# Two layers of a diffusion backbone: fp32 hidden blocks during selection and gates, and 96 expert rows fetched early

## The reference, cut to what matters

```python
q = (x @ wq).reshape(n, 8, 2, 128)
s = einsum('nhcd,hckd->nhck', q, sub_keys)      # 128 keys for each of 8 heads and 2 halves
s1, i1 = top_k(s[:, :, 0], 16); s2, i2 = top_k(s[:, :, 1], 16)
cand = (s1[..., :, None] + s2[..., None, :])    # 16 x 16 pairs
top, pos = top_k(cand, 16); idx = i1*128 + i2   # 16 experts of 16384 for each token and head
gate = softmax(top)
act = gelu(einsum('nd,nhkd->nhk', x, u_tab[idx]), approximate=False)
y = einsum('nhk,nhkd->nd', gate * act, v_tab[idx])
```

## Time and profile before

| | us |
|---|---|
| median of 3 runs (lowest, highest) | 5162.43 (5157.72, 5165.9) |
| the profiled execution | 5158.91 |
| its span | 5157.1 |

### The profile page before, as it was taken

One profiled execution on the slowest core, in us unless ns is written; L12 is line 12 of the kernel. 1 busy time (PEld: TensorE's weight loads), 2 busy tenths in 40 slices (PEclk: granted clock), 3 DMA queues, 4 the chain that ended last, 5 costly groups with the idle time before them and its releaser, 6 DMA issues. The chain is left out here.

```text
span 5157.1 us, 78818 instructions
## 1 busy us (share of the span) xinstructions
PE 4192.3 (81%) x29134; PEld 3640.1 (71%) x29134; DVE 3765.5 (73%) x6707; ACT 1603.1 (31%) x2322; POOL 1497.4 (29%) x1046
## 2 busy tenths in 40 slices
PE   6975996888788888888778579869887788888886
PEld 4944775888777777777668257759876777777775
DVE  2245664369997999999932567533999799999997
ACT  3133542323242222222231435232333322222223
POOL 0000000000005777777600000000000076777774
PEclk8986987999998999999989779789999999999998
DMA  5140001223379999999921400011334799999996
GB/s 195 61 158 12 2 2 35 78 82 124 106 224 362 408 409 409 406 409 409 361 67 49 154 4 2 2 69 49 116 122 144 244 401 409 409 403 409 409 409 249
DMA packets 398567, 1079.12 MB, mean 209 GB/s; under 512 B 37248, under 2 KB 176768, under 8 KB 394752
## 3 DMA queue, kind: packets, MB, share of 16 engines
q1 hardware_dynamic: 250880, 539.10, 29.2%
q0 software_dynamic: 147456, 536.94, 26.3%
HBM read 996.47 MB, written 79.43 MB: 209 GB/s over the span
## 5 line engine op out<-in xcount | busy, mean ns | idle before, releaser
L1912 POOL DMA_INDIRECT ring<-peer_u_rows,rows x512 | 732.1, 1430 | 2756.7 <-issue 1333.4
L196 PE MATMUL ps<-vhi,wlo 128*128 128x512 f32 x1536 | 655.5, 427 | 276.0 <-DVE wlo L2056 275.4
L1912 POOL DMA_INDIRECT ring<-peer_v,rows x512 | 743.1, 1451 | 252.0 <-DVE acc L2074 166.1
L196 PE MATMUL ps<-hhi,ulo 128*128 128x384 f32 x2048 | 713.4, 348 | 102.1 <-DVE ulo L1473 97.8
L198 PE MATMUL ps<-hhi,uhi 128*128 128x384 f32 x2048 | 701.7, 343 | 0.0
L197 PE MATMUL ps<-hlo,uhi 128*128 128x384 f32 x2048 | 701.4, 342 | 0.0
L2074 DVE SCALAR_TENSOR_TENSOR acc<-ring,act,acc 128x1024 f32<-128x1024 f32 x512 | 660.1, 1289 | 23.1 <-DMA ring<-peer_v,rows 3.4
L2065 DVE SCALAR_TENSOR_TENSOR ring<-ring,acc 128x1024 f32<-128x1024 f32 x512 | 620.2, 1222 | 55.7 <-DMA ring<-peer_u_rows,rows 48.6
L197 PE MATMUL ps<-vlo,whi 128*128 128x512 f32 x1536 | 644.5, 420 | 0.0
L198 PE MATMUL ps<-vhi,whi 128*128 128x512 f32 x1536 | 640.8, 417 | 0.0
L196 PEld LDWEIGHTS ps<-vhi,wlo 128*128 128x128 f32 x1536 | 317.4, 207 | 369.5 <-issue 292.0
(11 more groups left out here) (333 smaller groups left out, 7844.2 us busy)
## 6 DMA issues: line engine op xcount, KB each, us to landing
u<-peer_u SPq DMA_DIRECT2D x256, 512.0 KB
v<-peer_v SPq DMA_DIRECT2D x256, 512.0 KB
gates<-stage SPq DMA_DIRECT2D x24, 2048.0 KB, 9.6
gw<-gates SPq DMA_DIRECT2D x64, 768.0 KB
mod_ring<-mod_late SPq DMA_DIRECT2D x16, 2048.0 KB, 8.8
hidden<-hh SPq DMA_DIRECT2D x128, 192.0 KB, 1.9
ha<-hidden SPq DMA_DIRECT2D x128, 192.0 KB
proj_raw<-w_proj SPq DMA_DIRECT2D x42, 512.0 KB, 3.6
```

Of the source, the lines that this page charges most:

```text
L196: pe.matmul(out, lhs[1], rhs[0], start=start, stop=False)
L1912: pool.indirect_dma_start(ring[:, m % RING, :], None, table, rows).then_inc(row_in[m % RING], 16)
```

## The change

- `u` gets a ring of four slots (`U_RING`). In selection and gates the three fp32r products of a chunk become one plain fp32 product of the raw `u` and the raw normed tokens, which are kept as one fp32 tensor `h`. `u_high` and `u_low` are gone from both stages. `h2` lives only through the query stage; the experts stage splits `h` again into `x2` (384 tokens) at its start.
- From the second tile of selection on, GpSimd gathers 96 `peer_u` rows of the first gathered tile (`DOTS_AHEAD`, own ring of 8) and DVE multiplies them out, 24 in each of tiles 1 to 4, at places written out by hand (`dots`). The tokens are turned for that during tile 0 (`tokens_first`), on TensorE and ScalarE.
- The two reductions at line 1708 become halving additions of the one-hot tensor (8, 4, 2, then 1).
- The experts stage has 416 rows left, 13 in each turn. Rows of the two tiles alternate in the `peer_v` part (`row_of`), the first of them writes the accumulator (no memset), and DVE's 32 turns are written out instead of looped.

```diff
+        self.u = g.sb(st, "u", [P, U_RING, KC, P])
...
     def products(self, pe, slot, bank, chunks):
         for kc in chunks:
-            mm = split3(pe, self.g.ps[:, slot, 0:ND], [x[:, slot, kc, :] for x in self.u2],
-                        [x[:, kc, 0:ND] for x in self.g.h2], start=(kc == 0), stop=(kc == KC - 1))
+            mm = pe.matmul(self.g.ps[:, bank, 0:ND], self.u[:, slot, kc, :], self.x[:, kc, 0:ND], start=(kc == 0), stop=(kc == KC - 1))
...
+DOTS_AHEAD = 96
+SELECT_RING = 8
...
+        @block.gpsimd
+        def _(pool):
+            pool.wait_ge(listed, 1)
+            for m in range(DOTS_AHEAD):
+                if m >= SELECT_RING:
+                    pool.wait_ge(used, m - SELECT_RING + 1)
+                own.gather(pool, d["peer_u_rows"], 0, m, ring[:, m % SELECT_RING, :]).then_inc(row_in[m % SELECT_RING], 16)
...
             for t in range(TILES):
                 for p, n in blocks(t):
-                    hid.hidden(pe, n, n % 2, first=n < 2)
-                    if p == 1 and t >= 1:
+                    hid.hidden(pe, n, n // U_RING + 1, first=n < 2)
+                    if t == 0 and p in (1, 3):
+                        tokens_first(p // 2)
+                    if p == 3 and t >= 1:
                         turned(t - 1)
-                    if p == 3 and t + 1 < TILES:
+                    if p == 6 and t + 1 < TILES:
                         scores(t + 1)
...
-                    if p == 5:
+                    if p == 8:
                         act.wait_ge(dif, t + 1)
                         nc.scalar.activation(res[:, 2, :, :], res[:, 2, :, :], ACT.Exp).then_inc(ex, 1)
...
+            each_tile = DOTS_AHEAD // (TILES - 1)
+            def dots(t, a, b):
+                for m in range((t - 1) * each_tile + a, (t - 1) * each_tile + b) if t >= 1 else ():
+                    ve.wait_ge(row_in[m % SELECT_RING], 16 * (m // SELECT_RING + 1))
+                    own.dot(ve, ring[:, m % SELECT_RING, :], 0, m).then_inc(used, 1)
...
-                    if o == NO - 1:
-                        hid.u_low(ve, t + (N0 + 2), q)
...
+DOTS = SPARSE * P - DOTS_AHEAD
+ROWS = DOTS + SPARSE * P
+PER_TURN = ROWS // NG
+LEAD = 13
...
+def row_of(m):
+    if m < DOTS:
+        return divmod(DOTS_AHEAD + m, P)
+    m -= DOTS
+    if m < LEAD:
+        return 0, m
+    if m < 2 * P - LEAD:
+        half, x = divmod(m - LEAD, 2)
+        return x, half + LEAD * (1 - x)
+    return 1, m - P
```

More of the change, by code:

```diff
@@ L1512, in __init__, with gather, dot @@
         self.act = [g.sb(st, "act", [P, P]) for _ in range(SPARSE)]
+        self.acc = g.sb(st, "acc", [P, SPARSE, D])
+        self.g = g
     def row_numbers(self, ve, k, x, first, second, base):
         k.then(ve.scalar_tensor_tensor(self.act[x][:, :], first, float(NKEY), second, ALU.mult, ALU.add))
-        k.did(ve.tensor_scalar(self.rows[x][:, :], self.act[x][:, :], base, None, ALU.add))
+        k.then(ve.tensor_scalar(self.rows[x][:, :], self.act[x][:, :], base, None, ALU.add))
+    def gather(self, pool, table, x, slot, to):
+        rows = bass.IndirectOffsetOnAxis(self.rows[x][:, slot:slot + 1], 0)
+        return pool.indirect_dma_start(to, None, table, rows)
+    def dot(self, ve, row, x, slot):
+        return ve.scalar_tensor_tensor(row, row, 1.0, self.acc[:, x, :], ALU.mult, ALU.mult, accum_out=self.act[x][:, slot:slot + 1])
+DOTS_AHEAD = 96
+SELECT_RING = 8
 def select_stage(g, l, qT, sel, kt, loaded, hid, own):
@@ L1531, in select_stage @@
     lists = g.sem("sel_lists_done")
+    turned_h, tok_ready, listed, used = (g.sem(f"ahead_{x}") for x in ("h_turned", "h_ready", "rows_listed", "rows_used"))
+    row_in = [g.sem(f"ahead_gathered{i}") for i in range(SELECT_RING)]
+    g.gathers += row_in
     NC = 2 * PH
@@ L1752, in turns @@
         def turns(eng, body):
[L1754 to L1758, removed]
+            with eng.Fori(0, TG // U_RING - 1) as i:
+                for q in range(U_RING):
+                    body(i * U_RING + q, q, i, False)
+            for q in range(U_RING):
+                body(TG - U_RING + q, q, TG // U_RING - 1, True)
         @block.vector
@@ L1904, in _ @@
             tables = d["peer_u_rows"], d["peer_v"].rearrange("l i (j d) -> (l i j) d", d=D)
[L1905 to L1912, removed]
-                        m += 1
+            for m in range(ROWS):
+                if m >= RING:
+                    pool.wait_ge(used, m - RING + 1)
+                own.gather(pool, tables[m >= DOTS], *row_of(m), ring[:, m % RING, :]).then_inc(row_in[m % RING], 16)
         @block.sync
@@ L1993, in _, with x_high, u_high @@
         def _(act):
+            def x_high(half):
+                kc = slice(half * KC // 2, (half + 1) * KC // 2)
+                nc.scalar.activation(x2[0][:, kc, :], hid.x[:, kc, 0:ND], ACT.Copy).then_inc(x_hi, 1)
+            def u_high(i, b, first=False):
+                act.wait_ge(hid.u_in[b], i * 16 + 16 * (AHEAD // U_RING + 1))
+                if not first:
+                    act.wait_ge(hid.h_ready, i * 2 + (AHEAD + b - 1))
+                nc.scalar.activation(u2[0][:, b, :, :], hid.u[:, b, :, :], ACT.Copy).then_inc(u_hi, 1)
             def v_high(i, j):
@@ L2069, in value, with weights_of @@
-            def value(x):
-                def row(i, q):
-                    r = gathered(i, q)
-                    ve.wait_ge(used, i * PER_TURN + q)
-                    w = own.act[x][:, bass.ds((i - (SPARSE + x) * DOT_TURNS) * PER_TURN + q, 1)]
-                    ve.scalar_tensor_tensor(acc[:, x, :], r, w, acc[:, x, :], ALU.mult, ALU.add).then_inc(used, 1)
-                return row
-            def turn(i, last, row):
-                def rows(*which):
-                    for q in which:
-                        row(i, q)
+            def weights_of(x):
+                ve.wait_ge(acted, x + 1)
+                ve.tensor_tensor(own.act[x][:, :], own.act[x][:, :], own.share[x][:, :], ALU.mult).then_inc(shared, 1)
+                ve.wait_ge(shared, x + 1)
@@ new lines, in row @@
+            def row(m):
+                x, slot = row_of(m)
+                r = ring[:, m % RING, :]
+                if m >= DOTS and slot == 0:
+                    weights_of(x)
+                ve.wait_ge(row_in[m % RING], 16 * (m // RING + 1))
+                if m < DOTS:
+                    own.dot(ve, r, x, slot).then_inc(used, 1)
+                    return
+                w, acc = own.act[x][:, slot:slot + 1], own.acc[:, x, :]
+                ve.wait_ge(used, row_before(m) + 1)
+                if slot == 0:
+                    ve.tensor_scalar(acc, r, w, None, ALU.mult).then_inc(used, 1)
+                else:
+                    ve.scalar_tensor_tensor(acc, r, w, acc, ALU.mult, ALU.add).then_inc(used, 1)
@@ L2082, in turn, with rows @@
+            def turn(i, last):
+                at = iter(range(i * PER_TURN, (i + 1) * PER_TURN))
+                def rows(n):
+                    for _ in range(n):
+                        row(next(at))
                 v_low(i, 2)
-                rows(0, 1)
+                rows(1)
                 weigh(i, 2)
-                rows(2)
+                rows(1)
                 w_low(i, 2)
                 v_low(i, 3)
-                rows(3)
+                rows(1)
                 weigh(i, 3)
-                rows(4)
+                rows(1)
@@ L2110, in turn @@
                     w_low(i + 1, 0)
-                rows(14)
+                rows(1)
                 if not last:
                     w_low(i + 1, 1)
-                rows(15)
-            def weights_of(x):
-                ve.wait_ge(acted, x + 1)
-                ve.tensor_tensor(own.act[x][:, :], own.act[x][:, :], own.share[x][:, :], ALU.mult).then_inc(shared, 1)
+            x_low(0)
+            u_low(0, 0)
+            x_low(1)
+            u_low(0, 1)
             stores_done(ve)
@@ L2126, in _ @@
                 w_low(0, j)
-            ve.wait_ge(tok_ready, SPARSE)
-            with ve.Fori(0, DOT_TURNS) as i:
-                turn(i, False, dot(0))
-            with ve.Fori(DOT_TURNS, 2 * DOT_TURNS) as i:
-                turn(i, False, dot(1))
-            for x in range(SPARSE):
-                weights_of(x)
-            ve.wait_ge(used, SPARSE * P)
-            ve.memset(acc[:, :, :], 0.0).then_inc(shared, 1)
-            ve.wait_ge(shared, SPARSE + 1)
-            with ve.Fori(2 * DOT_TURNS, 3 * DOT_TURNS) as i:
-                turn(i, False, value(0))
-            with ve.Fori(3 * DOT_TURNS, LAST) as i:
-                turn(i, False, value(1))
-            turn(LAST, True, value(1))
+            for i in range(NG):
+                turn(i, i == LAST)
 def fold_stage(g, acc):
```

257 lines of the change are left out of this document (129 added, 128 removed).

## The result

The changed kernel takes 4928.4 us (median of 4 runs, 4923.23 to 4932.65) against 5164.16 before: a ratio of 0.9543, 95% interval 0.9531 to 0.9554, 236 us less. The forecast was 4936 us, range 4885 to 5012. The profiled execution has a span of 4923.9 us against 5157.1.

A forecast was written before the change was run, and what follows sets the result against it. It took DMA to bound the experts stage, with DVE close behind, and DVE to bound selection and gates. Experts -122, selection +21 and gates -11 make -112 us a layer, -224 for two: 4936 us, range 4885 to 5012.

The forecast's parts named there:

- inner range: Whole kernel: the forecast's own range from the bounds of experts, selection and gates a layer, given as 4890 to 4995 us.
- Experts: Experts stage: 13 rows instead of 16 cut a DMA-bound turn from 31.03 to 27.2 us, saving 122 us a layer.
- rival 4: Experts stage: DVE's written-out turns cost code fetches that eat the rows' gain, 2 us a turn, 5064 us; chance 0.05.
- Selection: Selection: dot products, halving additions and an Exp wait outweigh removed DVE work, 338 against 315.6 us, +21 us a layer.
- Wait for the Exp: Selection, tile 0: DVE waits 14 us for the Exp, now behind block 8 in ScalarE's order; no wait in later tiles.
- rival 2: Selection: gathers come late, at 3.3 us a row the stage grows by 38 us a layer, 5012 us; chance 0.05.
- Gates: Gates: twelve `u_low` go from DVE, 13.6 us, less 3 us for TensorE's first block at half clock: -11 us a layer.
- a cold start: Gates: TensorE enters with little to do before, its first block at half clock takes 10.6 us; 3 us allowed.
- The thin cover: Gates: TensorE needs 5.4 us of DVE's 5.69 us for a half tile, so DVE just covers it.
- rival 1: Experts stage: TensorE holds the turn at 29 to 31.2 us, its 4.3 us waits staying; 5116 us at 30; chance 0.07.
- rival 3: Selection: plain fp32 blocks at 1.2 GHz make TensorE set the pace, +242 us a layer, 5420 us; chance 0.03.

The follow-up runs named there:

- half the bytes of each row: Changed kernel with each experts-stage gather bringing 512 numbers of a row instead of 1024, used twice by DVE: 4840.7 us, 0.9377 of the kernel before.
- a quarter of DVE's work: Changed kernel with whole rows gathered in the experts stage but DVE using only the first 256 of 1024 columns: 4917.0 us, 0.9530 of the kernel before.
- Fp32 alone: Changed kernel with no rows fetched in selection, all 512 staying in the experts stage, 16 a turn: 5078.8 us, 0.9834 of the kernel before.
- the rows not in turn: Changed kernel with value rows going to one accumulator after the other instead of alternating: 4925.7 us, 0.9537 of the kernel before.
- the Exp early: Changed kernel with tile 0's Exp behind block 5 instead of block 8 in ScalarE's order: 4905.6 us, 0.9504 of the kernel before.

## Why the prediction was right

The time came out 8 us under the forecast, and each stage changed in the way and for the reason that the sum gives. That the whole is so near is in part luck: in layer one the experts stage gave 4 us less than foretold, selection cost 4.5 us less and the gates gave 3 us more, and these misses cancel in part. The inner range was added up wrongly: its bounds give 4900 to 5004, not 4890 to 4995. Nothing hangs on it, since the measured time lies inside both.

- *Experts, -122 foretold, -118 measured.* The mechanism was right: the stage follows its bytes (half the bytes of each row -44 us, a quarter of DVE's work -4 us a layer). The term that was too large is the turn. The 31 turns from the first load of `gw` to the last took 962.0 us before and 851.3 after, 31.03 and 27.46 us each, so a turn saved 3.57 us and not 3.83, 111 us and not 119. What lies outside them saved 7.4 us, not 4. I had set the new turn at 27.2 us by the 408 GB/s of the middle of the stage; over all 31 turns the rate was 404 GB/s, 406 before. DVE at 1.4 us behind is not the reason: with a quarter of its row work the same turns still take 27.34 us each. Fp32 alone shows a reason that I had put at nothing: with all 512 rows the rebuilt stage takes 31.29 us a turn instead of 31.03, and lasts 6.6 us longer. The kernel with the rows not in turn, as fast as the changed one, speaks against the alternation; what is left is the turns written out (rival 4) and the other edits of the stage. In those 31 turns the instruction queue of the DMA engines (q14) moved 16 packets where it moved 8 before, which fits rival 4, but no run separates it, so this cause stays open. The rate stayed at 407 GB/s from 1600 to 2400 us beside a DVE busy 95% of the time.
- *Selection, +21 foretold, +16.5 measured (+14.6 in layer two).* Wait for the Exp: 14 us foretold, 9.7 measured. The block of plain fp32 was taken at 5.3 us from merged rows of another shape; 16 records of 0.323 us make 5.17, and turning the tokens kept PE busy for 1.04 instead of 1.8 us each. The halving additions took 3.3 us a tile (1110.17 to 1113.43 us in the kernel with the Exp early), against 3 taken. Tiles 2 and 3 lasted 69.0 us each against some 70; the windows of tiles 0 and 2:

```profile
1078.06:1131.98 53.92, 53.92 (x200) 33.81 (x200) 43.22 (x225) 11.20 (x15) 0.33 (x1) 1.00 0.42 121
...
1202.45:1271.44 68.99, 63.76 (x213) 38.60 (x212) 68.68 (x271) 10.42 (x16) 25.98 (x24) 0.95 0.87 294
```

  In layer one DVE waits for a row once in this stage, for 0.3 us, so rival 2 did not come. POOL needed 25.98 us for 24 gathers in tile 2, 1.08 us each, beside a DVE busy 68.68 of 68.99 us, and DVE waited for none of them. SBUF — State Buffer in the Trainium skill ("SBUF: two separate sides") has GpSimd unable to write descriptors while DVE runs an operation in a two-port mode; the trace doesn't name the mode of an instruction, but whatever GpSimd lost to it here delayed nothing.
- *Gates, -11 foretold, -13.9 and -15.1 measured.* The twelve `u_low` alone are 13.6 us. I had kept 3 us for a cold start. It came, and cost nothing that shows: TensorE enters the stage at half clock (0.50 from 1411.26 to 1416.00 us, and likewise in layer two), while DVE is still at its casts before the first half tile. The 1.3 us between the two layers (146.5 against 145.2) lie at the other end, where the last 48 bf16 products took 4.24 us at a clock of 0.66 in layer one and 2.93 us at 1.00 in layer two. The thin cover held: DVE starts a half tile every 5.67 us (1420.92, 1426.59), and TensorE does its work in the same time:

```profile
1423.82 2.80 PE L1464 MATMUL ps<-h,u 128*128 128x384 f32 x8
1426.73 2.92 PE L1833 MATMUL ps<-ob,oa 128*128 128x128 bf16 x48
1429.49 2.80 PE L1464 MATMUL ps<-h,u 128*128 128x384 f32 x8
```

- *The rivals.* TensorE's wait for `w_low` shrank from 4.3 to about 2 us a turn and its clock rose from 0.92 to 0.97, so rival 1 did not come. Rival 3, the slow selection, needed a clock of 0.65 and found 0.94; but the experiment with fp32 alone shows its mechanism at full clock: without rows in the stage, TensorE's blocks do set selection. The slack that I gave with rival 3 (a block may take 6.0 us) was made by the dot products. Rival 4 was not tried by itself; the 8 us a layer by which the turns of fp32 alone are longer than before are the most that is left for it, against the 64 that I had priced.

## What to carry to other kernels

Where a stage is held by transfers and the one before it by an engine, price a move by what each stage really lacks: bytes in the first (0.52 MB is 1.28 us at 408 GB/s), engine time in the second (1.15 us), less the time in which that engine would have waited. Three cheap fp32r products against one plain fp32 product is not TensorE's choice alone: here the plain one costs TensorE 1.0 us a block and gives back 1.14 us of DVE, which was the engine that counted. Moving a small instruction (the Exp) in the order of a third engine was worth another 23 us, found as the one long wait left on the bounding engine. And an experiment that takes back the main part of a change (here the early rows) also prices the rest of it: 6.6 us a layer of the rebuilt stage were hidden in the gain.

## What the runs showed of the hardware that was not expected

The granted clock of TensorE was at its upper level of 2.4 GHz (1.00) for the whole 285 us of selection with fp32 alone, where PE was busy 284.07 us, and 0.93 in the mean before, where it waited for the low parts:

```profile
PE ps L196 <- DVE ulo L1473: 48.1, 34, 1.9
```

Its busy time in the stage rose from 256.27 to 284.07 us, 28 us, where the product times at full clock (5.17 against 4.15 us a block) say 53 us for 52 blocks. So plain fp32 cost TensorE less here than the ratio of its product times says; that the clock is the whole difference was not tested by itself.
